# 8x8 blocks of a delta-rule head: matrices ahead of scaled values, strips read back on two queues, the next head's decay rows in a buffer of their own

## The reference

```python
diff = gc[..., :, None] - gc[..., None, :]            # gc: running sum of the log decays
decay_incl = jnp.exp(jnp.where(incl, diff, -jnp.inf))
decay_strict = jnp.where(strict, decay_incl, 0.0)
lmat = jnp.einsum('nbhcd,nbhed->nbhce', kb, k) * decay_strict
tmat = triangular_solve(lmat + eye, eye)              # inverse of a unit lower triangular matrix
u_base = jnp.einsum('nbhce,nbhef->nbhcf', tmat, v * beta[..., None])
qk = jnp.einsum('nbhcd,nbhed->nbhce', q, k) * decay_incl
```

## Time and profile before

| | us |
|---|---|
| median of 3 runs | 2058.17 (2056.67 to 2069.95) |
| the profiled execution | 2066.66 |
| its span on the core | 2064.9 |
| PE busy in it | 2005.1 (97%) |
| DVE busy | 1296.5 (63%) |
| ACT busy | 903.4 (44%) |
| POOL busy | 190.3 (9%) |
| chain that ended last: PE / DMA / ACT / DVE | 78% / 11% / 5% / 3% |

### The profile page before, as it was taken

How to read it: one execution, slowest core, us unless ns; L and a number is a source line. 1 busy time by engine, 2 the same in 40 slices (tenths; PEclk the granted TensorE clock), 3 DMA queues, 4 the chain that set the end, 5 groups by cost and what they waited for, 6 DMA issues and landing times.

```text
span 2064.9 us, 46675 instructions
## 1 busy us (share of the span) xinstructions
PE 2005.1 (97%) x16811; PEld 1940.0 (94%) x16811; DVE 1296.5 (63%) x2430; ACT 903.4 (44%) x1908; POOL 190.3 (9%) x351
## 2 busy tenths in 40 slices
PE   9999999999999999999899999999999999999998
PEld 8988888988898998888889999999999999999998
DVE  5877777777677777777745445555556656754433
ACT  6454544455444455455543334333333333433343
POOL 5210111111111111111100000000000000000010
PEclk9999999999999999999999999999999999999999
DMA  8554555554455554455554454444544444444443
GB/s 248 161 151 121 140 163 157 141 163 131 130 164 158 153 160 123 136 156 166 164 163 153 132 163 161 156 151 147 167 155 141 153 152 160 148 158 147 145 140 113
DMA packets 425032, 314.70 MB, mean 152 GB/s; under 512 B 63529, under 2 KB 421242, under 8 KB 424698
## 3 DMA queue, kind: packets, MB, share of 16 engines
q1 hardware_dynamic: 378648, 305.74, 48.3%
q10 hardware_dynamic: 46322, 8.14, 2.1%
HBM read 285.48 MB, written 29.22 MB: 152 GB/s over the span
## 4 chain that ended last, share of the span: by engine, by line
PE 78%; DMA 11%; ACT 5%; DVE 3%; ACTq 2%; issue 1%; SPq 0%; DVEq 0%
PE ps L318 24%; PE ps L320 23%; PE ps L319 23%; PE ps L1300 7%; DMA l_blocks<-lmat 3%; DMA xc<-x_blocks 3%; DMA n<-l_blocks 2%; DMA x_blocks<-n 1%; ACT dec_t L699 1%; ACTq L780 1%; ACT whi L300 1%; DVE n L1144 1%; ACTq L758 1%; DVE t L1139 1%; ACT convout L729 1%
## 5 line engine op out<-in xcount | busy, mean ns | idle before, releaser
L318 PE MATMUL ps<-xhi,whi 128*128 128x320 f32 x3072 | 990.2, 322 | 4.0 <-DVE zraw L964 1.1
L320 PE MATMUL ps<-xhi,wlo 128*128 128x320 f32 x3072 | 957.6, 312 | 0.0
L319 PE MATMUL ps<-xlo,whi 128*128 128x320 f32 x3072 | 957.3, 312 | 0.0
L305 DVE TENSOR_TENSOR wlo<-wraw,whi 128x1024 fp32r<-128x1024 f32 x480 | 581.0, 1232 | 179.4 <-ACT whi L300 176.9
L300 ACT ACTIVATE whi<-wraw 128x1024 fp32r<-128x1024 f32 x480 | 496.6, 1055 | 433.5 <-PE ps L320 295.5
L318 PEld LDWEIGHTS ps<-xhi,whi 128*128 128x128 f32 x3072 | 583.4, 190 | 28.5 <-issue 18.9
L319 PEld LDWEIGHTS ps<-xlo,whi 128*128 128x128 f32 x3072 | 584.9, 190 | 1.2
L320 PEld LDWEIGHTS ps<-xhi,wlo 128*128 128x128 f32 x3072 | 584.0, 190 | 0.0
L318 PE MATMUL ps<-bhi,whi 128*128 128x320 f32 x512 | 157.7, 308 | 0.0
L319 PE MATMUL ps<-blo,whi 128*128 128x320 f32 x512 | 157.6, 308 | 0.0
L320 PE MATMUL ps<-bhi,wlo 128*128 128x320 f32 x512 | 157.6, 308 | 0.0
(11 more groups left out here) (350 smaller groups left out, 1966.1 us busy)
## 6 DMA issues: line engine op xcount, KB each, us to landing
wraw<-in_delta_w_in_dram SPq DMA_DIRECT2D x384, 256.0 KB, 3.2
wraw<-in_pool_w_in_dram SPq DMA_DIRECT2D x256, 256.0 KB, 3.1
wraw<-in_delta_w_out_dram SPq DMA_DIRECT2D x128, 256.0 KB, 3.3
wraw<-in_pool_w_out_dram SPq DMA_DIRECT2D x128, 256.0 KB, 3.2
s_s<-in_state_delta_dram SPq DMA_DIRECT2D x32, 512.0 KB, 5.9
out_dram<-s_s SPq DMA_DIRECT2D x32, 512.0 KB, 4.2
wraw<-in_pool_w_group_dram SPq DMA_DIRECT2D x64, 256.0 KB, 3.1
dec<-gc_rows SPq DMA_DIRECT2D x16, 320.0 KB, 4.7
```

The lines of the kernel that those rows point to most:

```text
L305: nc.vector.tensor_tensor(wlo[:, slot, :], wraw[:, slot, :], whi[:, slot, :].bitcast(F32), ALU.subtract).then_inc(E("w_lo"), 1)
L318: mm(o, whi[:, slot, w], hi[:, k_x, :], start=first, stop=False)
L319: mm(o, whi[:, slot, w], lo[:, k_x, :], start=False, stop=False)
L320: done = mm(o, wlo[:, slot, w], hi[:, k_x, :], start=False, stop=last)
```

## The change

- `lmat` (line 1118) moves ahead of `vb`, the sums of line 1110 and, in the last head, `split(0)`.
- Of the four strips read back into `xc`, ACT issues two and SP two. SP's two stand ahead of piece 10, behind a wait for `x_out`.
- The decay rows land in a new buffer `dec_in`; DVE writes the exponents from it to `dec`, POOL reads it. `decays(i)` now waits for `diff` (the exponents of the head before) in place of `l_mat`, and stands ahead of piece 2 (piece 6 for the second head) in place of piece 11 (10). `decay_exponents` no longer waits for `hidden`.

```diff
@@ -141,6 +141,7 @@
     ngc = place(a, "ngc", [5])
     kept = a[0]
     kq_m = place(a, "kq_m", [4 * P + 32])
+    dec_in = place(a, "dec_in", [5, P])
     n8 = place(a, "n8", [64])
     t8 = place(a, "t8", [16])
     pc = place(a, "pc", [TILE_LEVELS - 1, 5, BL])
@@ -371,7 +372,7 @@
                  one_block(j % 4, w_in, PK * (j % 4), i * 256 + (2 * DM if j < 8 else QKV)))
 
         def decays(d):
-            sp.dma_start(dec[:].rearrange("p u c -> p (u c)"),
+            sp.dma_start(dec_in[:].rearrange("p u c -> p (u c)"),
                          gc_dram.rearrange("r c -> (r c)")[bass.ds(d * (5 * P), 5 * P)].partition_broadcast(P)
                          ).then_inc(E("dec_landed"), 16)
 
@@ -399,6 +400,12 @@
             for q, c0 in enumerate((i * P, i * P + DM, i * 256 + 2 * DM, i * 256 + (2 * DM + P))):
                 sp.dma_start(s_rows[:, bass.ds(c0, P)], cc_out[32 * q:32 * q + 24, :]).then_inc(E("cc_dma"), 16)
                 sp.dma_start(p_rows[:, bass.ds(c0, P)], cc_out[32 * q + 24:32 * q + 27, :]).then_inc(E("cc_dma"), 16)
+
+        def strips_back(n):
+
+            sp.wait_ge(E("x_out"), n * 16 + 16)
+            for h in range(2, 4):
+                sp.dma_start(xc[BL * h:BL * h + BL, :, :], strip_blocks(x_dram, h)).then_inc(E("x_in"), 16)
 
         for j in range(2):
             head_piece(0, HEADS, j)
@@ -428,7 +435,9 @@
         cache_store(0)
         for j in range(4, 12):
             if j == 10:
-                sp.wait_ge(E("l_mat"), 1)
+                strips_back(1)
+            if j == 6:
+                sp.wait_ge(E("diff"), 1)
                 sp.wait_ge(E("hidden"), 1)
                 decays(1)
             head_piece(1, HEADS + 12, j)
@@ -436,6 +445,10 @@
             sp.wait_ge(E("cc_t"), i)
             cache_rows(i)
             for j in range(12):
+                if j == 2:
+                    sp.wait_ge(E("diff"), i)
+                    sp.wait_ge(E("hidden"), i)
+                    decays(i)
                 if j == 4:
                     cache_store(i - 1)
                 if j == 5:
@@ -443,11 +456,8 @@
                 if j == 6:
                     sp.wait_ge(E("delta_out"), i * 48 - 32)
                     states_in(i - 1)
-                if j == 11:
-
-                    sp.wait_ge(E("l_mat"), i)
-                    sp.wait_ge(E("hidden"), i)
-                    decays(i)
+                if j == 10:
+                    strips_back(i)
                 head_piece(i, i * 12 + HEADS, j)
 
         early = ht[:, 0:EARLY, :].rearrange("p k t -> p (k t)")
@@ -465,6 +475,8 @@
                 sp.wait_ge(E("tail"), NH)
                 sp.wait_ge(E("gate"), NH)
                 sp.dma_start(early, ht_dram[:, 0:EARLY * T]).then_inc(E("ht_in"), 16)
+            if j == 10:
+                strips_back(NH)
             load(sp, OUT_A + j, j % 4, one_block(j % 4, w_out, PK * (j % 4), 256 * (j // 4)))
 
         sp.wait_ge(E("cc_dma"), 128 * NH)
@@ -549,8 +561,8 @@
             pool.wait_ge(E("dec_landed"), i * 16 + 16)
             if not isinstance(i, int) or i:
                 pool.wait_ge(E("at"), i)
-            gp.tensor_tensor(dec_t[:, 0:4, :], dec[:, 0:4, :], wide_row(hide_p, 4), ALU.add)
-            gp.tensor_tensor(dec_t[:, 4, :], dec[:, 4, :], hide_s[:], ALU.add).then_inc(E("hidden"), 1)
+            gp.tensor_tensor(dec_t[:, 0:4, :], dec_in[:, 0:4, :], wide_row(hide_p, 4), ALU.add)
+            gp.tensor_tensor(dec_t[:, 4, :], dec_in[:, 4, :], hide_s[:], ALU.add).then_inc(E("hidden"), 1)
 
         pool.wait_ge(E("table"), 1)
         pool.wait_ge(E("c_all"), 1)
@@ -776,7 +788,7 @@
             act.dma_start(small_blocks(x_dram), n8[0:80, :].rearrange("p (r c) -> p r c", c=8)).then_inc(E("x_out"), 16)
             split(5)
             act.wait_ge(E("x_out"), n * 16 + 16)
-            for h in range(4):
+            for h in range(2):
                 act.dma_start(xc[BL * h:BL * h + BL, :, :], strip_blocks(x_dram, h)).then_inc(E("x_in"), 16)
             split(6)
             act.wait_ge(E("ksqs_ps"), n)
@@ -1054,9 +1066,8 @@
 
             dve.wait_ge(E("next"), i * 2 + 2)
             dve.wait_ge(E("dec_landed"), i * 16 + 16)
-            dve.wait_ge(E("hidden"), i + 1)
             for u in range(5):
-                last = v.scalar_tensor_tensor(dec[:, u, :], dec[:, u, :], gc_next[:, u:u + 1],
+                last = v.scalar_tensor_tensor(dec[:, u, :], dec_in[:, u, :], gc_next[:, u:u + 1],
                                               mask_p[:] if u < 4 else mask_s[:], ALU.add, ALU.add)
             last.then_inc(E("diff"), 1)
 
@@ -1101,22 +1112,21 @@
                                 small[:, 21:23].rearrange("p (o c) -> p o c", o=1).to_broadcast([P, 2, 2]), ALU.mult)
             v.tensor_scalar(scaled[:, :, 4], betas[:, :, 4], small[:, 23:24], None, ALU.mult).then_inc(E("nb"), 1)
 
-            dve.wait_ge(E("qkv_ps"), n * 3 - 1)
-            dve.wait_ge(E("hb"), n)
-            v.tensor_tensor(vb[:, 0:4, :], blocks(D0, 4), wide(hb[:, 0:4], 4), ALU.mult)
             dve.wait_ge(E("kk_ps"), n)
-            v.tensor_scalar(vb[:, 4, :], D3[:, 384:512], hb[:, 4:5], None, ALU.mult)
-            dve.wait_ge(E("squares"), n * 2)
-            v.tensor_scalar(small[:, 0:3], small[:, 54:57], float(P), 4 * P * EPS, ALU.mult, ALU.add).then_inc(E("sums"), 1)
-
-            if quarter:
-                split(0)
             dve.wait_ge(E("dec"), n)
             dve.wait_ge(E("nb"), n)
             for u in range(5):
                 kk = D2[:, 256 * (u % 2) + P:256 * (u % 2) + 256] if u < 4 else D3[:, P:256]
                 last = v.scalar_tensor_tensor(lmat[:, u, :], kk, nb[:, u:u + 1], dec[:, u, :], ALU.mult, ALU.mult)
             last.then_inc(E("l_mat"), 1)
+            dve.wait_ge(E("qkv_ps"), n * 3 - 1)
+            dve.wait_ge(E("hb"), n)
+            v.tensor_tensor(vb[:, 0:4, :], blocks(D0, 4), wide(hb[:, 0:4], 4), ALU.mult)
+            v.tensor_scalar(vb[:, 4, :], D3[:, 384:512], hb[:, 4:5], None, ALU.mult)
+            dve.wait_ge(E("squares"), n * 2)
+            v.tensor_scalar(small[:, 0:3], small[:, 54:57], float(P), 4 * P * EPS, ALU.mult, ALU.add).then_inc(E("sums"), 1)
+            if quarter:
+                split(0)
             if quarter:
                 quarter(2)
                 split(1)
```

## The result

| | before | after |
|---|---|---|
| median, us | 2060.85 (2056.67 to 2069.95) | 2001.1 (1999.77 to 2003.21) |
| span of the profiled execution | 2064.9 | 1998.1 |
| mean granted clock | 0.984 | 1.000 |
| PE busy | 2005.1 | 1980.7 |

What follows compares the result with a forecast made beforehand. PE, busy 97%, loses time only waiting for the transpose and to clock drops; 38.3 us of waits plus 21 of clock give 59, so 1999 to 2007.5, forecast 2004 (likeliest case 1996 to 2016; wider range 1994 to 2034).

Steps and rivals of the forecast that it cites:

- The sum: Whole profiled span: 38.3 of PE's 43.1 us of waiting go and 21 of clock loss return, together 59 us.
- A: `lmat` ahead of `vb` on DVE: ends 1.3 us sooner, strips land 1.2 sooner a head (bounds 0 to 1.4).
- B: Strips read back on ACT and SP, ahead of piece 10: 1.01 us of issue, plus 0 to 1.2 of landing.
- DVE's floor: DVE's convolution step ahead of the transpose limits the read-back's gain to DVE's idle time there, 1.58 us in head 6.
- C: Decay rows in `dec_in`, loaded earlier on SP: nothing held up, POOL's masks run earlier, head 1 gains 1.2 us.
- the cover that the prediction named: POOL's masks beside `gate` and `split(3)` cost DVE up to 1.1 us, but nothing if over before the blocks are read.
- the 1.61 of head 7: PE's wait for the transpose in head 7 brought no clock drop, so waits under 1 us should bring none.
- Only one lever works: Strips of `lmat` land no sooner or read-back keeps its latency: 33 us saved, 2025; chance 20%.
- no change: Both ends of the chain to the transpose are swallowed, waits stay near 2.4 us: 2050 to 2060; chance 6%.
- slower: The write of `lmat` meets the state loads and waits grow by 2.2 us a head: 2090; chance 5%.
- More than forecast: No PE wait and no clock drop at all: 43.1 + 24 us off, 1994 from the median; chance 7%.

Runs made afterwards that it cites:

- A and B: Changed kernel with the decay rows in `dec` again, loaded ahead of piece 11 behind SP's two strips: 2001.17 us, ratio to before 0.9699.
- B without A: Changed kernel with `lmat` back behind the scaled values `vb`: 2016.83 us, ratio to before 0.9777.
- two sums: Changed kernel with two unused 128x640 sums on DVE ahead of the transpose, transfers untouched: 2038.23 us, ratio to before 0.9899.
- A alone: Kernel before with only `lmat` moved ahead of the scaled values: 2038.24 us, ratio to before 0.9871.
- C alone: Kernel before with only the decay rows in their own buffer and loaded half a head sooner: 2031.64 us, ratio to before 0.9847.
- three sums: Changed kernel with three unused 128x640 sums on DVE ahead of the transpose, transfers untouched: 2062.56 us, ratio to before 1.0011.
- four sums: Changed kernel with four unused 128x640 sums on DVE ahead of the transpose, transfers untouched: 2079.90 us, ratio to before 1.0103.

## Why the prediction was right

**The bound and the size.** The one wait of PE was the whole matter, as table 1 shows. The sum was 59 us; the medians differ by 59.8 and the two profiled spans by 66.8. The prediction halved the 8.5 us between the profiled execution and the median; with the profiled span at 1998.1 in place of 2006, the sum on the profile's own basis was 8 us short. Before rounding that is 7.5 (66.8 less 59.3). It splits into 3.2 of waiting (1.6 us stay, 4.8 were forecast), 3.4 of clock (PE's busy time falls by 24.4, 21 were forecast), and 0.9 in the rest of PE's idle time. That 2004 stands only 3 us from the median is therefore partly luck: the kernel before lost less in its median execution than in the profiled one.

**A: the step was oversized.** The issue moved by the 1.3 forecast, 0.03 behind `lmat`. The landing moved by 0.70 only (columns 1 and 2: 9.93 to 9.23), where 1.2 was taken "near the top, since the first issue follows `lmat` alone". That reason was about the issue and says nothing of the landing. The text had named the traffic that takes part of it back, and in the new place the DMA share is 1.03, against 0.92 while the last strip was under way before. Which transfer takes the 0.6 was not tested.

**B: undersized in what it offers, right in what is used.** The read-back is done 3.14 us sooner, against at most 2.2 by the bounds (1.01 of issue, 1.2 of landing). The floor of the landing, the block read's 2.92, was wrong: the four strips each land within 1.7 to 2.1 us when nothing larger stands ahead of them, and the two in the middle had shown 2.9 to 3.0 because piece 10 ran beside them (1.9 with it held back). The prediction said that the trace has no strip without the other traffic; but the first of the four, issued 0.4 us ahead of piece 10, landed in 1.70 us in the mean of heads 2 to 15, and the shortest landing of a strip in the kernel before was there to read (us, min/median/max):

```profile
DMA to landing us min/median/max: 1.6/3.0/5.0
```

What saved the number is DVE's floor. The prediction said that the transpose can gain at most DVE's idle time there beyond what `lmat` gives; it had 1.58 in head 6, and the mean is 29.6 / 16 = 1.85, or 1.74 over heads 2 to 15 alone. Measured in heads 2 to 15 (column 6): 2.52 in sum, with 2.6 forecast. 0.70 of it is what the strips of `lmat` land sooner, by A, and the other 1.82 is the work of B and C. Two errors, 0.5 too much and 0.4 too little, hide each other.

**One queue or two.** With nothing larger ahead of them a strip took 1.8 us on one queue and 1.7 and 2.0 on two, and the second queue brought 0.73 of the 3.36 us: by columns 4 and 5 the last strip is issued 0.93 sooner and takes 0.20 longer. The Trainium skill (*DMA: Bandwidth & Descriptors*, "Rules for kernel authors") has the rule that spreading transfers over queues saves only the issuing engine's time; these numbers bear it out. The result that the prediction drew from it, a sum 3 us smaller, did not follow, since it left out what B does beside that: it puts the strips ahead of two large transfers.

**C: costed at nothing, and right only in company.** With A and B in place C is worth nothing (2001.17 against 2001.10). Alone it is worth about 30 us, since it takes the broadcast out of the last strip's way, as the prediction had said of B ("both go behind the strips or away") without seeing that either part does it. Behind B without A it costs 6 us. The masks also did not run "right behind `at`" (line 1138, 374.40) but 2 us later, since POOL was still at its own powers and products, at lengths of 1.75 and 2.00 us. The first of them waits for the sums (line 1127), which A has moved behind `lmat`; without A the masks started 0.14 us behind `at`. So they met neither `gate` nor `split(3)`, which ended at 376.27, and the cost of 1.1 us that the prediction allowed for did not arise there:

```profile
372.50 1.75 POOL L594 TENSOR_TENSOR small<-small,minushalf 128x3 f32<-128x3 f32 x1 [1.70 <-DVE small L1127]
374.33 2.00 POOL L596 TENSOR_TENSOR small<-small,cur 128x4 f32<-128x4 f32 x1
376.29 0.18 POOL L599 TENSOR_TENSOR small<-small,cur 128x1 f32<-128x1 f32 x1
376.43 1.29 POOL L564 TENSOR_TENSOR dec_t<-dec_in,hide_p 128x512 f32<-128x512 f32 x1
```

The masks end at 378.14, ahead of the blocks' landing at 380.7, so the cover that the prediction named held. `split(6)` takes 1.2 us as forecast.

**The clock.** That waits under 1 us bring no drop held in every run; the 1.61 of head 7 as a mark for safety did not, since with two sums heads 8 and 9 dropped behind 1.57 and 1.55 us. The price was right for the kernel before: 24.4 us of busy time for 41.5 us of waiting, 1.6 us of span for each us waited. It is a price per drop more than per us. Over the changed kernel's 1980.7, PE's busy time rises by 1.6 to 1.8 us for each head with a drop: 14 such heads in the kernel before, 8 in A alone, 5 in C alone, 7 and 14 with two and three sums; only four sums cost more, 2.05 in each of 14. So each us waited cost from 1.4 (C alone) to 1.6 us of span.

**Head 16** kept 1.5 us in place of 3.2. The write of `lmat` lands 1.6 us after its issue there, not 6.4. The state loads now start behind it (951.51, its last issue 949.86), where they had started just ahead of it (1010.61, its first issue 1010.94); no run separates this from the other traffic there. What remains slow are the block read (about 6) and the write of the blocks:

```profile
960.71 5.96 DMA x_blocks<-n
966.69 0.36 ACTq L792
967.05 0.04 issue
967.09 2.11 DMA xc<-x_blocks
```

**The rivals.** "Only one lever works" (2025), "no change" and "slower" fell. "More than forecast" fell as a time, 1994 against 2001.1, but its account, no wait and no drop at all, is nearer to what the two profiles show than the forecast is: 67 us on its side, 59 on the forecast's, 66.8 measured. The levers replace each other rather than add: alone they take off 1.3, 2.5 and 1.5%, in sum 5.3, together 3.0, because there was no more to win than one wait. That is also why the forecast was safe: any two of the three parts give at least 2.2%.

## What to carry to other kernels

When a chain of small transfers sets a wait, look at what is issued to any queue just ahead of each link or among its transfers: moving one weight load behind them was worth more here (1.21 us) than the second queue (0.73). Price a wait of the busiest engine with what the clock adds behind it, and test that price by delaying the event on purpose. When several edits shorten one wait, count what is left to win once, and find out by which of them the others become needless.

## What the runs showed of the hardware

- In the means of heads 2 to 15, a 20 KB strip takes 1.7 to 2.1 us from issue to landing with nothing larger ahead of it. It takes about 3.0 beside a weight piece (two transfers of 256 KB) issued a little ahead or just behind it on another queue, 2.65 right behind the piece on the same queue, and 4.25 (the last of four) with a 320 KB broadcast besides.
- Where the DMA engines were full (a share of 1.03 in head 6), issuing 1.3 us sooner landed 0.7 us sooner.
- The length of a wait does not settle whether the clock falls: 2.12 us without and 1.55 with a drop in one trace, 2.97 without (A alone, head 1). Behind a wait for the transpose of under 1.5 us it never fell in these 13 traces.
- Each head with a drop costs PE 1.6 to 1.8 us of busy time; with waits of 3.2 to 4.0 us (four sums) it is 2.05.
- POOL's small operations stretch beside DVE: line 596 takes 2.00 us in the changed kernel's head 6 and 0.20 in the kernel without A, while DVE's rows beside it keep their length; with the masks on `split(3)` both sides took longer (1.74 and 1.94). In which cases which side gives way was not tested.
